# Expert value rows gathered by token and summed on TensorE in its four 32-column pieces

## What is computed

```python
pre  = einsum('thkd,td->thk', expert_u[experts], xb)
coef = gate * gelu(pre)
out  = einsum('thk,thkd->td', coef, expert_v[experts])
x    = layer_norm(ALPHA * h + out)
```

## Time and profile before

| | us |
|---|---|
| three runs | 2463.3, 2464.38, 2469.81 |
| median | 2464.38 |
| profiled execution, from first to last instruction | 2466.4 |
| PE busy | 1859.5 |
| DVE busy | 1654.0 |
| POOL busy | 1346.2 |
| ACT busy | 438.2 |

### The profile page before, as it was taken

The page is one execution under the profiler, slowest core; times in us unless marked ns, Lnnn a source line. Parts: engine busy times, 40 slices in busy tenths (PEclk is TensorE's granted clock), DMA queues, the critical chain, the costliest instruction groups (busy, mean ns, idle before and its releaser), DMA issues. The chain is left out here.

```text
span 2466.4 us, 23548 instructions
## 1 busy us (share of the span) xinstructions
PE 1859.5 (75%) x6595; PEld 906.3 (37%) x6598; DVE 1654.0 (67%) x3363; ACT 438.2 (18%) x1063; POOL 1346.2 (55%) x1174
## 2 busy tenths in 40 slices
PE   8998998979949674247766767776677886666796
PEld 6766654735426331012222222332224352222231
DVE  2114886698797894898998475598445559855544
ACT  0122543101011211010202021222121121111120
POOL 1100000257767664755446366775865757777775
PEclk9998997999969897568888889998989998899999
DMA  4105330799989997999999999999999999899997
GB/s 184 64 12 163 103 120 1 279 350 358 410 297 406 351 337 256 402 376 388 387 384 394 385 382 386 397 353 342 381 397 375 410 397 374 320 390 409 410 401 306
DMA packets 258180, 791.69 MB, mean 321 GB/s; under 512 B 30562, under 2 KB 55203, under 8 KB 257347
## 3 DMA queue, kind: packets, MB, share of 16 engines
q0 software_dynamic: 166400, 604.58, 63.8%
q1 hardware_dynamic: 90692, 180.59, 20.8%
q10 hardware_dynamic: 960, 5.03, 0.5%
HBM read 783.90 MB, written 5.59 MB: 320 GB/s over the span
## 5 line engine op out<-in xcount | busy, mean ns | idle before, releaser
L1214 PE MATMUL ps<-arena 128*128 128x512 f32 (+1 forms) x1632 | 838.6, 651 | 296.7 <-DMA arena<-peer_v,arena 253.6
L820 POOL DMA_INDIRECT arena<-peer_u,arena x576 | 683.6, 1187 | 670.6 <-DVE arena L1823 317.9
L1860 DVE CUSTOM_DVE_ANT_0 arena<-arena 128x1024 f32<-128x1024 f32 x576 | 693.9, 1226 | 377.3 <-DMA arena<-peer_u,arena 368.7
L820 POOL DMA_INDIRECT arena<-peer_v,arena x576 | 643.2, 1117 | 299.2 <-issue 153.0
L1214 PEld LDWEIGHTS ps<-arena 128*128 128x128 f32 (+1 forms) x1632 | 300.5, 199 | 778.0 <-issue 622.5
L1869 DVE SCALAR_TENSOR_TENSOR arena<-arena 128x1024 f32<-128x1024 f32 x163 | 209.7, 1286 | 108.8 <-DMA arena<-peer_v,arena 104.6
L1512 ACT ACTIVATE arena<-arena 128x128 f32<-128x128 f32 (+1 forms) x408 | 150.6, 393 | 681.4 <-PE ps L1214 672.9
L1037 PE MATMUL ps<-arena 128*128 128x448 f32 (+2 forms) x512 | 159.4, 472 | 24.2 <-DVE arena L1763 23.3
L1069 PE MATMUL ps<-arena 128*128 128x128 f32 (+2 forms) x768 | 147.1, 352 | 2.6 <-ACT arena L1400 2.3
L849 PE MATMUL ps<-arena 128*128 128x296 f32 (+1 forms) x512 | 131.3, 417 | 10.6 <-DMA arena<-w_proj 10.6
L1190 PE MATMUL ps<-arena 128*64 128x512 f32 (+1 forms) x512 | 94.5, 518 | 57.1 <-DMA arena<-v_b 57.1
(11 more groups left out here) (192 smaller groups left out, 1630.6 us busy)
## 6 DMA issues: line engine op xcount, KB each, us to landing
arena<-k_b SPq DMA_DIRECT2D x128, 256.0 KB
arena<-v_b SPq DMA_DIRECT2D x128, 256.0 KB
arena<-w_mix SPq DMA_DIRECT2D x56, 512.0 KB, 6.6
arena<-w_q SPq DMA_DIRECT2D x48, 512.0 KB, 6.7
arena<-kv_a SPq DMA_DIRECT2D x128, 128.0 KB
arena<-w_out SPq DMA_DIRECT2D x24, 512.0 KB, 6.7
arena<-peer_u,arena POOLq DMA_INDIRECT x576, 9.2
arena<-peer_v,arena POOLq DMA_INDIRECT x576, 7.5
```

The lines of the kernel that those rows point to most:

```text
L820: pool.indirect_dma_start(out=rows[slot_of[n]], out_offset=None, in_=io["peer_v"] if v else io["peer_u"], in_offset=bass.IndirectOffsetOnA ...
L1214: last = pe.matmul(bank(6 + a, 512, 0, nt), diag_p[read_before[n] % ND][:, 0:nt], rows[slot_of[n]][:, a * 512:(a + 1) * 512], start=(k == ...
L1860: dve.tensor_tensor_reduce(out=row, in0=row, in1=h, scale=1.0, scalar=0.0, op0=ALU.mult, op1=ALU.add, accum_out=pre[:, k:k + 1]).then_inc( ...
```

## The change

A value gather now takes one token instead of one pick: the 128 picks of that token lie on the partitions. So the sum over picks is a product with the token's coefficient column. All 576 value blocks go to TensorE; VectorE has none, and `facc`, the diagonals and the fold are gone.

- The picks and the coefficients of a tile are transposed by TensorE in columns 384 and up of bank 4 ("ids_t", "coef_t"), copied by ScalarE, and the picks turned back into whole numbers by VectorE ("ids_u").
- `strips` is sixteen strips of 64 columns of zeros, set once by POOL. ScalarE writes the coefficient columns of eight tokens ("strip") into column 31 of eight of them. A window of 32 columns over a strip puts that column at any of 32 places; the other 31 add zero. The token is thus one row of a 32-row piece of the output.
- Gathers go to the pieces in turn (`token_of`): token 0, 32, 64, 96, 1, 33 and so on; the tile of 64 uses two pieces. Each block is two products of 32 columns by 512, one after the other in the same piece.
- No value block of a tile can be summed ahead of the transposed coefficients of the whole tile. So the order of gathers is another: u of tile 0, its values, all 128 of u of tile 1, then u of tile 2 woven with 120 values, u of tile 3 with 124, 60 values alone, u of tile 4 with 64, the rest. Positions of the sample attention stay; "route" of tiles 2 and 3 comes 60 places earlier, and "finish" 0 moves from place 259 to 257, ahead of "ix" 1 at 258.
- "iy" uses bank 5 alone, and products in bank 4 wait for the copies of the transposes.

```diff
-        lead = [(0, 0, k) for k in range(NE)] + [(0, 1, k) for k in range(NE)] + [(1, 0, k) for k in range(64)]
...
+        us = [[(i, 0, k) for k in range(rows_of[i])] for i in range(5)]
+        vs = [[(i, 1, k) for k in range(TOKENS[i])] for i in range(5)]
+        later = vs[1] + vs[2] + vs[3]
+        gathers = us[0] + vs[0] + us[1] + weave(us[2], later[:120]) + weave(us[3], later[120:244]) + later[244:304]
+        gathers += weave(us[4], later[304:368]) + later[368:] + vs[4]
...
+        def token_of(i, k):
+
+            return 32 * (k % LANES[i]) + k // LANES[i]
...
-                pe.wait_ge(dp_ready, read_before[n] + 1)
+                if k % GT == 0:
+                    pe.wait_ge(strip_ready, G + 1)
                 pe.wait_ge(row_loaded[slot_of[n]], 16 * fill_of[n])
+                lhs = strips[:, GT * (G % 2) + k % GT, MID - r_:MID - r_ + 32]
                 for a in range(2):
-                    last = pe.matmul(bank(6 + a, 512, 0, nt), diag_p[read_before[n] % ND][:, 0:nt],
-                                     rows[slot_of[n]][:, a * 512:(a + 1) * 512],
-                                     start=(k == pe_first[i]), stop=(k == pe_last[i] and i < 4))
+                    last = pe.matmul(bank(6 + a, 512, 32 * lane, 32 * lane + 32), lhs, rows[slot_of[n]][:, a * 512:(a + 1) * 512],
+                                     start=(r_ == 0), stop=(r_ == 31))
                 last.then_inc(pe_used, 1)
...
+            def turned_ids(i):
+
+                act.wait_ge(xt_ready, turn_no["ids_t", i] + 1)
+                if i:
+                    act.wait_ge(idsT_ready, i)
+                act.activation(idsTF[:, 0:TOKENS[i]], bank(4)[:, 384:384 + TOKENS[i]], ACT.Copy).then_inc(xt_copied, 1)
...
+            def strip(i, j):
+
+                G, L = GROUP0[i] + j, LANES[i]
+                if G < 2:
+                    act.wait_ge(strips_zeroed, 1)
+                else:
+                    act.wait_ge(pe_used, GT * (G - 1))
+                n = GT // L
+                src = coefT[i % 2][:, 0:TOKENS[i]].rearrange("p (l r) -> p r l", l=L)[:, n * j:n * j + n, :]
+                dst = strips[:, GT * (G % 2):GT * (G % 2) + GT, MID].rearrange("p (r l) -> p r l", l=L)
+                act.activation(dst, src, ACT.Copy).then_inc(strip_ready, 1)
...
-                    dve.tensor_tensor(facc, facc, ps[:, 6 * 512:6 * 512 + D], ALU.add).then_inc(vacc_read, 1)
-                    dve.wait_ge(vacc_read, i + 1)
-                    step(dve.scalar_tensor_tensor(v, v, ALPHA, facc, ALU.mult, ALU.add))
...
+                dve.wait_ge(pe_used, GT * (GROUP0[i] + GROUPS[i]))
+                dve.scalar_tensor_tensor(v, v, ALPHA, ps[0:nt, 6 * 512:6 * 512 + D], ALU.mult, ALU.add).then_inc(vacc_read, 1)
```

More of the change, by code:

```diff
@@ L444, in program, with weave @@
-        gathers += vs[nv:]
-        gathers += [(4, 1, k) for k in range(NPACK)]
+        TOKENS = [nt for _, nt in MTILES]
+        LANES = [nt // 32 for nt in TOKENS]
+        def weave(us, vs):
+            out, nv = [], 0
+            for n, u in enumerate(us):
+                out.append(u)
+                while nv < len(vs) * (n + 1) // len(us):
+                    out.append(vs[nv])
+                    nv += 1
+            return out
+        us = [[(i, 0, k) for k in range(rows_of[i])] for i in range(5)]
@@ L458, in program @@
[L458 to L461, removed]
+        by_dve = [v == 0 for _, v, _ in gathers]
+        GROUPS = [nt // GT for nt in TOKENS]
+        GROUP0 = [sum(GROUPS[:i]) for i in range(5)]
         due = [[] for _ in range(NG + 1)]
+        where = {}
@@ L556, in program, with between @@
                 n = gather_at[i, 0, k1 - 1]
[L557 to L565, removed]
+                last = k1 == rows_of[i]
+                put(max(n + (1 if last else 3), 44 if i == 0 else 0), "gelu", i, g)
+                put(max(n + (3 if last else 6), 47 if i == 0 else 0), "coefs", i, g)
+        bank4 = [(where["mix", p, m], where["mixed", p, m]) for p in (1, 2) for m in range(KD)]
+        bank4 += [(where["s_score", q, 4], where["s_exp", q]) for q in range(NB)]
+        bank4 += [(where["out", 1, 0], where["turn", 3])]
+        def between(n):
+            while any(a <= n < b for a, b in bank4):
+                n += 1
+            return n
+        sum_at, turned_at = {}, []
+        for i in range(5):
+            at = between(gather_at[i, 0, 0] + (40 if i == 0 else 60 if i < 4 else 20))
+            put(at, "ids_t", i)
+            put(at + 3, "ids_u", i)
+            turned_at.append(between(gather_at[i, 0, rows_of[i] - 1] + 4))
+            put(turned_at[i], "coef_t", i)
+        for i in range(5):
+            for k in range(TOKENS[i]):
+                if k % GT == 0:
+                    G = GROUP0[i] + k // GT
+                    put(max(turned_at[i], sum_at[G - 2] + 1 if G >= 2 else 0), "strip", i, k // GT)
+                n = gather_at[i, 1, k]
+                at = max(n + 1, turned_at[i] + 1)
+                put(at, "sum", n)
+                sum_at[GROUP0[i] + k // GT] = at
+            if i < 4:
+                put(at + 1, "finish", i)
+                put(at + 9, "store", i)
         plan = list(pre_items)
@@ L1067, in query @@
                     pe.wait_ge(qp_copied, n - 1)
+                if p and n % 2 == 0:
+                    turned_before("query", p, m)
                 for k in range(KD):
@@ L1217, in add_row @@
                 last.then_inc(pe_used, 1)
-            def fold():
-                pe.wait_ge(dve_used, n_dve)
-                for a in range(2):
-                    last = pe.matmul(bank(6 + a, 512, 0, NTAIL), const("fold_s"), facc[:, a * 512:(a + 1) * 512],
-                                     start=False, stop=True)
-                last.then_inc(folded, 1)
             project()
```

194 lines of the change are left out of this document (118 added, 76 removed).

## The result

The changed kernel takes 2498.18 us (median of 4 runs, 2494.64 to 2505.74), the kernel before 2467.1 beside it (2463.3 to 2471.32): ratio 1.0132, 95% interval 1.011 to 1.0155, slower by 31 us. The profiled execution has a span of 2492.9 us.

What follows compares the result with a forecast made beforehand. Transfers were taken to bound the kernel, with at most 107 us to win. 53 - 15 - 2 = +36 on the profile's 2466.4 gave 2502.4, less 2 for the median: 2500; own range 2485 to 2515 (chance 0.40), full range 2450 to 2560.

Steps and rivals of the forecast that it cites:

- VectorE's value rows are worth nothing by themselves: Whole gather part: 163 additions of 1.286 us, 210 us in all, leave VectorE without gaining time.
- A value row costs TensorE 0.86 us: Value sums on TensorE: a row's four records hold the queue for two rounds, 0.86 us, between bounds 0.43 and 1.71.
- The query part: Between gathers 128 and 256: sixteen query products with four value sums behind each, 143 us in all, +34 us.
- full-overlap rival: Value rows on four pieces overlap fully, 0.43 us a row; query part 115 us, end 2478; chance 0.15.
- Gather 256 is 33 us late: End of gathers 128 to 256: gather 256 issued some 33 us late, at 958; finish 0 begins at 970.
- Keys and admission: Sampler on tile 1: last key scores at about 878, index keys end 27 us later, admit at 1004 instead of 981.
- The 28 us stall costs nothing more when it goes: Before admit: POOL's 28.39 us wait, 15 us of idle transfers, goes; this only takes up part of the delay.
- VectorE binds gathers 256 to 384: The u run: VectorE needs 263 us from admit to the reading of gather 384; +53 us, delay of 33 included.
- 384 to the end, -15: From gather 384 on: 15 of 37 us of idle transfer time given back, through VectorE's routing and TensorE's faster late rows.
- the fold, -2: At the end: the fold, four records in 1.88 us, goes; last row, finish and store stay; -2 us.
- The faster rival: VectorE does not bind the u run, its work from admit to 384 at most 214 us; end 2432; chance 0.16.
- The strict order: Only a row's last record overlaps the next row's first, 1.28 us a row; end 2526; chance 0.17.

Runs made afterwards that it cites:

- experiment 1: Kernel before with one edit each: the new gather order alone, 2557.21 against 2518.97 us, ratio 1.017; the finish of tile 0 earlier alone, 2451.4 against 2465.47, ratio 0.9927.
- experiment 2: Kernel before with new gather order and early finish, values summed as before: 2537.48 against 2518.36 us, ratio 1.0096; second run 2555.67 against 2528.99, ratio 1.0112.

## Why the prediction was right, and where its steps were not

Forecast 2500, measured 2498.18: the sum was +36 us, measured +31. Step by step:

- *VectorE's value rows are worth nothing by themselves.* In agreement: 216 us less work, and no stretch where it gave time back is shown. (They were 168, not 163: the first of each tile stands on a line of its own, 0.76 us each.)
- *A value row costs TensorE 0.86 us.* Wrong, twice over. In fours it costs 0.49, near the floor of 0.43. The weight loads go as I had read them, eight at once and then four at a time, but a row does not hold the queue for its two rounds: the rows behind it run in the same rounds. Alone between scores it costs 1.83 (856.12 to 857.95). The query part runs at 7.25 us a query (7.2 by the full-overlap rival, 8.9 by mine). The lone rows behind it, which I had at 0.86 or under transfers, took back what the fours had saved.
- *Gather 256 is 33 us late.* It was 13.6 late, and finish 0 began at 953.63, not 970. Gathers 128 to 256 took 230.67 us, outside the 240 to 255 that were to show the forecast right.
- *Keys and admission.* The last scores stand at 872.58 (878 forecast), the key loads begin 7 us after them in both kernels and end at 984.5 (987 forecast), the admission is at 1007.22 (1004), and 21 u rows are read between the finish and it, as counted. The working has the keys 27 us later but the admission only 23 (1004 against 981); both were some 22 (984.5 against 962.3, and 1007.22 against the 984.84 of the key-bound kernel of experiment 1). So the mis-sized row did no harm: the two errors on TensorE nearly offset each other ahead of the last scores. That was luck.
- *The 28 us stall costs nothing more when it goes.* Wrong. Experiment 1 prices it at 14 us of median (18 by the ratio) in the kernel before, and experiment 2 at 0.74% with the new order. I took the key-bound admission for the bound of the stretch, but transfers that idled were lost whatever waited for the keys. The sum escaped this error because its terms were absolute times of the changed kernel, which has no stall. Split into causes by the ratios, an estimate over chips of both kinds, the change is about -18 us (finish), +42 to +46 (order), +5 to +10 (sums), and not +36 with the stall at nothing.
- *VectorE binds gathers 256 to 384.* Right, and the largest term: 263 us from admission to the read of gather 384 were forecast and 259.1 taken (1267 and 1266.34). VectorE is 88% busy against my nine tenths. The stretch took 310.8 us (about 300 forecast). The share is 0.91, above the 0.85 that I gave: 1.01 over the 68 us ahead of the admission, and still 0.88 behind it. The GB/s column shows the loss more plainly. Both kernels moved 101 MB from gather 256 to 384 (325 x 310.82, 359 x 280.76). At the 409 GB/s of the earlier trace rows that is 247 us, so by this estimate the transfers lost 64 us here (60 forecast) and 34 before, and that is the 30 us between the two.
- *384 to the end, -15, and the fold, -2.* Measured -17 together, but as -22 and +5. Of my two reasons for the first, the order seems to be most of it and the sums little (experiment 2); the new order with the values on VectorE was not measured on the faster chips. The +5 was not foreseen. The fold went, but the last row is summed 13.5 us after its gather was issued, where it had landed after 6.4 us before; by the page a value row lands after 10.5 us in the median, 7.5 before. That the two parts add up to the forecast was luck.
- *The faster rival* needed VectorE's job at 214 us or less; it did 259.1. *The strict order* did not occur. The Trainium skill, "TensorE: Matmul & The Clock Gate", Part 3, says that products start and end in program order. The trace does not agree for this form: records of four rows on different column pieces started together (16 in 1.95 us, 7.07 in one piece), ahead of earlier rows' later records. So the cost that I drew from that rule was wrong here.

## What to carry to other kernels

A change that takes work off an engine may force an order on the rest. Here value rows by token can only start when all coefficients of their tile are there, so 128 u rows come in one run, and the engine that was relieved on average becomes the bound of that run; look for the longest stretch of one kind of work before looking at averages. Then move the movable work of that engine out of the run: moving two kinds of it won back all that the change lost. And price a stall by the transfers that idle in it, in its own experiment, even if the next known wait seems to cover it.

## What the runs showed of the hardware

- Products of 32 columns overlap across the four column pieces and not within one: 1.95 and 7.07 us for 16 records of 512 columns. The granted clock was 0.96 and 0.97 over gathers 128 to 256 in these two kernels. From 256 to 384, with TensorE a third busy (36%), it was 0.64.
- Chips differ more than most effects here: the kernel before takes 2465.47 us on one and 2518.97 on another, and 96 key loads of 32 KB beside the gathers take 103 to 105 us on the faster kind and 118 to 136 on the slower. An edit whose effect hangs on those keys measures differently on each.
- A gather's issue on GpSimd took 1.28 us on average in the run of u rows (gathers 288 to 383). In the trace of the changed kernel the 292 issues during which VectorE did nothing took 0.94 us each, none over 0.95, and the 135 that lay at least nine tenths within VectorE's 1.2 us operations on rows took 1.51 on average. No run varied one of the two alone.
